# Two-block transformer forward pass in split fp32, one core: the attention bias masked once in its table, and the end of the second block's mixer in another order

## What is computed

```python
for l in range(DEPTH):                                   # first block, DEPTH = 2
    x = x + 0.5 * swiglu(rms_norm(x, ffn1_norm[l]), ffn1_w_in[l], ffn1_w_out[l])
    x = x + mixer(rms_norm(x, mix_norm[l]), ...)         # neighbourhood attention + Fourier mix
    x = x + 0.5 * swiglu(rms_norm(x, ffn2_norm[l]), ffn2_w_in[l], ffn2_w_out[l])

# in the neighbourhood attention: a learned bias per head and offset, and a mask by column
s = einsum(q, k_win) * scale + bias
s = where(col_ok, s, -inf)

for l in range(DEPTH):                                   # second block
    y_a = mla_attention(...)                             # group 0
    y_b = short_gated_conv(...)                          # group 1
    y_c = multiscale_pool(...)                           # group 2
    y_d = swa_sink_attention(...)                        # group 3
    gf = groups * rsqrt(mean(groups * groups) + eps)     # one mean per group of 256 channels
    x = x + (gf * mix_norm) @ w_o[l]
    x = x + (silu(gate) * up) @ w_down[l]
```

## Time and profile before

| | |
|---|---|
| three runs | 1720.05, 1720.64, 1723.21 us, median 1720.64 |
| profiled execution, first to last instruction | 1721.5 us |
| PE busy | 1671.8 us (97%) |
| DVE busy | 943.5 us (55%) |
| ACT busy | 803.8 us (47%) |
| POOL busy | 97.1 us (6%) |
| mean granted TensorE clock | 0.990 |

### The profile page before, as it was taken

How to read it: one execution, slowest core, us unless ns; L and a number is a source line. 1 busy time by engine, 2 the same in 40 slices (tenths; PEclk the granted TensorE clock), 3 DMA queues, 4 the chain that set the end, 5 groups by cost and what they waited for, 6 DMA issues and landing times.

```text
span 1721.5 us, 22066 instructions
## 1 busy us (share of the span) xinstructions
PE 1671.8 (97%) x7760; PEld 1376.7 (80%) x7760; DVE 943.5 (55%) x843; ACT 803.8 (47%) x899; POOL 97.1 (6%) x105
## 2 busy tenths in 40 slices
PE   6999999999999999999999999899999999999998
PEld 5887887888888787888888888787888878788886
DVE  4545545575545645465566545566554556665454
ACT  5443454544434543444455444465444446544443
POOL 2010000010000002000001000021100002110000
PEclk9999999999999999999999999999999999899999
DMA  8875453446565578555345655644456564336552
GB/s 259 295 221 175 172 190 123 139 156 199 176 208 188 175 251 240 174 173 181 111 152 166 203 188 194 240 127 129 141 190 200 179 195 144 125 127 201 189 192 89
DMA packets 209187, 308.96 MB, mean 179 GB/s; under 512 B 10400, under 2 KB 153504, under 8 KB 208480
## 3 DMA queue, kind: packets, MB, share of 16 engines
q1 hardware_dynamic: 208272, 305.18, 54.1%
q0 software_dynamic: 560, 1.84, 0.4%
q10 hardware_dynamic: 288, 1.05, 0.2%
HBM read 306.97 MB, written 2.88 MB: 180 GB/s over the span
## 4 chain that ended last, share of the span: by engine, by line
PE 90%; DVE 3%; ACT 3%; issue 2%; DMA 1%; POOL 1%; DVEq 0%; SPq 0%; ACTq 0%; POOLq 0%
PE pg L1380 19%; PE pg L1381 18%; PE pg L1382 18%; PE acc L1382 9%; PE acc L1380 9%; PE acc L1381 9%; PE pg L1451 2%; DVE wlo L970 2%; ACT whi L671 1%; DMA raw<-in_ffn_w_in 1%; PE pg L1393 1%; PE acc L1530 1%; PE acc L1550 1%; POOL ms L590 0%; PE acc L1538 0%
## 5 line engine op out<-in xcount | busy, mean ns | idle before, releaser
L970 DVE TENSOR_TENSOR wlo<-raw,whi 128x2048 fp32r<-128x2048 f32 x277 | 641.2, 2316 | 513.8 <-ACT whi L671 513.8
L671 ACT ACTIVATE whi<-raw 128x2048 fp32r<-128x2048 f32 x277 | 529.5, 1913 | 338.6 <-PE pg L1382 168.2
L1380 PE MATMUL pg<-whi,xTh 128*128 128x512 f32 (+1 forms) x1456 | 580.3, 399 | 9.9 <-DVE wlo L970 5.7
L1382 PE MATMUL pg<-whi,xTl 128*128 128x512 f32 (+1 forms) x1456 | 570.4, 392 | 0.0
L1381 PE MATMUL pg<-wlo,xTh 128*128 128x512 f32 (+1 forms) x1456 | 570.2, 392 | 0.0
L1380 PEld LDWEIGHTS pg<-whi,xTh 128*128 128x128 f32 x1456 | 276.3, 190 | 73.6 <-DVE wlo L970 9.8
L1382 PEld LDWEIGHTS pg<-whi,xTl 128*128 128x128 f32 x1456 | 276.0, 190 | 57.5
L1381 PEld LDWEIGHTS pg<-wlo,xTh 128*128 128x128 f32 x1456 | 276.5, 190 | 54.3
L1380 PE MATMUL acc<-whi,bTh 128*128 128x512 f32 (+1 forms) x572 | 229.6, 401 | 0.0
L1382 PE MATMUL acc<-whi,bTl 128*128 128x512 f32 (+1 forms) x572 | 224.3, 392 | 0.0
L1381 PE MATMUL acc<-wlo,bTh 128*128 128x512 f32 (+1 forms) x572 | 223.1, 390 | 0.0
(11 more groups left out here) (159 smaller groups left out, 1048.2 us busy)
## 6 DMA issues: line engine op xcount, KB each, us to landing
raw<-in_ffn_w_in SPq DMA_DIRECT2D x176, 512.0 KB, 4.8
raw<-in_ffn_w_out SPq DMA_DIRECT2D x88, 512.0 KB, 4.0
raw<-in_w_gate_up SPq DMA_DIRECT2D x88, 512.0 KB, 4.7
raw<-in_mix_w_in SPq DMA_DIRECT2D x64, 512.0 KB, 4.1
raw<-in_w_down SPq DMA_DIRECT2D x44, 512.0 KB, 4.0
raw<-in_w_in SPq DMA_DIRECT2D x24, 512.0 KB, 4.8
raw<-in_mix_w_o SPq DMA_DIRECT2D x16, 512.0 KB, 4.7
raw<-in_w_o SPq DMA_DIRECT2D x16, 512.0 KB, 4.5
```

The costliest lines, as they stand in the source:

```text
L671: act_e.activation(whi[:, slot, :], raw[:, slot, :], ACT.Copy).then_inc(s.w_hi_ready, 1)
L970: v.tensor_tensor(wlo[:, slot, :], raw[:, slot, :], f32(whi[:, slot, :]), ALU.subtract).then_inc(s.w_lo_ready, 1)
L1380: pe.matmul(dst, xh, wh, start=first and i == 0, stop=False)
L1382: mm = pe.matmul(dst, xl, wh, start=False, stop=last and i == len(pairs) - 1)
```

## The change

The column mask is added to the table `rpb_spread` in memory, once for both layers, by seven more software DMAs that add while they write (`mask_table`). GpSimd issues them after the first norm. SP waits for them before it copies the window, and DVE now waits for the copy itself. GpSimd's addition in SBUF is gone from both layers.

In the second block's mixer the order is changed on all engines. PE attends `sw` unit 2 ahead of `pool_mix`, transposes `pair_T(0, 0)` inside half block 7 and `pair_T(0, 1)` inside `project(0, 0)`, and attends `mla` unit 2 behind `project(0, 0)`. ACT and DVE follow: the refill of unit 12 moves from the front of the `mla` exp to behind `pair_hi(0, 1)`, `scale_pair` is taken tile by tile, and `mla_out(1)` comes behind the refill of unit 12. The transposes of k = 0 use other PSUM banks.

```diff
 def attention_bias():
-    sp.wait_ge(s.rpb_spread, LOADED * NA_DR)
+    sp.wait_ge(s.rpb_masked, LOADED * NA_DR)
...
+def mask_table():
+    mask = bass.AP(tensor=a["consts_a"].tensor, offset=CA_MASK, ap=[[0, DEPTH * NA_H], [CA_COLS, GRID_W], [1, GRID_W]])
+    pool.wait_ge(s.rpb_spread, LOADED * NA_DR)
+    for dr in range(NA_DR):
+        pool.dma_start(spread[:, :, dr * GRID_W:(dr + 1) * GRID_W].rearrange("q h k -> h q k"), mask,
+                       accum_op=ALU.add).then_inc(s.rpb_masked, LOADED)
 spread_table()
+norm(0)
+mask_table()
...
-    pool.wait_ge(s.bias_landed, 64 * l + 64)
-    pool.wait_ge(s.consts_a_landed, 16 * l + 16)
-    pool.tensor_tensor(flat, flat, consts_a[:, CA_MASK:].unsqueeze(1).to_broadcast([P, TT * NA_H, T]),
-                       ALU.add).then_inc(s.bias_masked, 1)
...
 # ACT, end of mixer_b
 group_square(0, 3, 0, s.sw_o_sb, 2 * l + 1)
+group_square(1, 3, 1, s.sw_o_sb, 2 * l + 2)
 refills(11)
-group_square(1, 2, 0, s.pool_sb, l + 1)
-group_square(2, 2, 1, s.pool_sb, l + 1)
+group_square(2, 2, 0, s.pool_sb, l + 1)
+group_square(3, 2, 1, s.pool_sb, l + 1)
 mla_probs_T(1)
-group_square(3, 3, 1, s.sw_o_sb, 2 * l + 2)
-refills(12)
+group_square(4, 0, 0, s.mla_o_sb, 2 * l + 1)
+pair_hi(0, 0)
 mla_exp(2)
 out_gate_copy(1)
 mla_probs_T(2)
-group_square(4, 0, 0, s.mla_o_sb, 2 * l + 1)
-pair_hi(0, 0)
 pair_hi(0, 1)
+refills(12)
+group_square(5, 0, 1, s.mla_o_sb, 2 * l + 2)
 refills(13)
-group_square(5, 0, 1, s.mla_o_sb, 2 * l + 2)
...
 # DVE, end of mixer_b
 mla_out(0)
+sw_out(1)
 (pool scale)
 refills(11)
-sw_out(1)
+scale_pair(0, 0)
 mla_max(2)
+scale_pair(0, 1)
+pair_lo(0, 0)
+conv_in(1)
+pair_lo(0, 1)
 refills(12)
-conv_in(1)
-scale_pair(0)
 mla_out(1)
-pair_lo(0, 0)
-pair_lo(0, 1)
 refills(13)
 (conv gate)
-scale_pair(1)
+scale_pair(1, 0)
+scale_pair(1, 1)
 refills(14)
 pair_lo(1, 0)
```

More of the change, by code:

```diff
@@ L142, in __init__ @@
         self.rpb_spread = sem("rpb_spread")
+        self.rpb_masked = sem("rpb_masked")
         self.bias_landed = sem("bias_landed")
@@ L416, in build, with pair_bank @@
         pairs_b = ((2, 3), (0, 1))
-        def pair_bank(t):
-            return (acc[2], pg[1][0])[t]
+        def pair_bank(k, t):
+            return ((pg[1][0], acc[1]), (acc[2], pg[1][0]))[k][t]
         out_b = ((pg[0][0], acc[3]), (acc[1], acc[0]))
@@ L608, in spread_table @@
                             .then_inc(s.rpb_spread, LOADED)
+            def mask_table():
+                mask = bass.AP(tensor=a["consts_a"].tensor, offset=CA_MASK, ap=[[0, DEPTH * NA_H], [CA_COLS, GRID_W], [1, GRID_W]])
+                pool.wait_ge(s.rpb_spread, LOADED * NA_DR)
+                with nc.allow_non_contiguous_dma(reason="rows of 64 keys"):
+                    for dr in range(NA_DR):
+                        pool.dma_start(spread[:, :, dr * GRID_W:(dr + 1) * GRID_W].rearrange("q h k -> h q k"), mask,
+                                       accum_op=ALU.add).then_inc(s.rpb_masked, LOADED)
             pool.wait_ge(raw_landed[1], 2 * LOADED)
             spread_table()
+            norm(0)
+            mask_table()
             with pool.Fori(0, DEPTH) as l:
-                norm(3 * l)
-                pool.wait_ge(s.bias_landed, 64 * l + 64)
-                pool.wait_ge(s.consts_a_landed, 16 * l + 16)
-                flat = bias.rearrange("p t h k -> p (t h) k")
-                pool.tensor_tensor(flat, flat, consts_a[:, CA_MASK:].unsqueeze(1).to_broadcast([P, TT * NA_H, T]),
-                                   ALU.add).then_inc(s.bias_masked, 1)
                 norm(3 * l + 1)
@@ L625, in _ @@
                 norm(3 * l + 2)
-            norm(6)
+                norm(3 * l + 3)
             with pool.Fori(0, DEPTH) as l:
@@ L899, in pair_hi @@
                     act_e.wait_ge(s.tr_done, 4 * (o + 1) + 2 * k + t + 1)
-                    act_e.activation(xTh[:, 4 * half:4 * half + 4, tok(t)], pair_bank(t)[:, :].rearrange("p (c n) -> p c n", c=4),
+                    act_e.activation(xTh[:, 4 * half:4 * half + 4, tok(t)], pair_bank(k, t)[:, :].rearrange("p (c n) -> p c n", c=4),
                                      ACT.Copy).then_inc(s.xT_hi_ready, 1)
@@ L1081, in mixer_a @@
                 refills(7)
-                v.wait_ge(s.bias_masked, l + 1)
+                v.wait_ge(s.bias_landed, 64 * l + 64)
                 v.wait_ge(s.gate_bias_landed, 32 * l + 32)
@@ L1279, in conv_in, with scale_pair @@
                         .then_inc(s.z_ready, 1)
-                def scale_pair(k):
+                def scale_pair(k, t):
                     v.wait_ge(s.grstd_ready, 2 * l + k + 1)
[L1284 to L1289, removed]
+                    for i, g in enumerate(pairs_b[k]):
+                        c = slice(g * GD, (g + 1) * GD)
+                        last = v.scalar_tensor_tensor(xn[:, t, c], y[:, t, c], g_r[:, k, 2 * t + i:2 * t + i + 1], gain_m[:, c],
+                                                      ALU.mult, ALU.mult)
+                    last.then_inc(xn_ready[t], 1)
                 def pair_lo(k, t):
@@ L1294, in pair_lo @@
                     v.wait_ge(s.xT_hi_ready, 4 * (o + 1) + 2 * k + t + 1)
-                    v.tensor_tensor(xTl[:, part, tok(t)], pair_bank(t)[:, :].rearrange("p (c n) -> p c n", c=4),
+                    v.tensor_tensor(xTl[:, part, tok(t)], pair_bank(k, t)[:, :].rearrange("p (c n) -> p c n", c=4),
                                     f32(xTh[:, part, tok(t)]), ALU.subtract).then_inc(s.xT_lo_ready, 1)
@@ L1321, in mixer_b @@
                 refills(11)
[L1322 removed]
+                v.wait_ge(s.gain_m_landed, 16 * (DEPTH + 1) + 16 * l + 16)
+                scale_pair(0, 0)
                 mla_max(2)
+                scale_pair(0, 1)
+                pair_lo(0, 0)
+                conv_in(1)
+                pair_lo(0, 1)
                 refills(12)
[L1325 to L1327 removed]
                 mla_out(1)
[L1329 to L1330 removed]
                 refills(13)
@@ L1786, in pool_mix, with pair_T @@
                     mm.then_inc(s.unit_done, 1)
+                def pair_T(k, t):
+                    half = 1 - k
+                    if k == 0 and t == 0:
+                        pe.wait_ge(s.z_ready, 2 * l + 1)
+                        pe.wait_ge(s.out_gate_sb, 2 * l + 1)
+                    if k == 0 and t == 1:
+                        pe.wait_ge(s.sw_biased, 3 * l + 3)
+                    pe.wait_ge(xn_ready[t], 2 * (o + 1) + k + 2)
+                    for c in range(4):
+                        at = (4 * half + c) * P
+                        tr = pe.transpose(pair_bank(k, t)[:, c * P:(c + 1) * P], xn[:, t, at:at + P], ident[:, :])
+                    tr.then_inc(s.tr_done, 1)
                 for i in range(8):
@@ L1791, in mixer_b @@
                     u = (6, 9)[b] + half
-                    mm = half_block(t, half, u % SLOTS, rnd + u // SLOTS, BANK, pg[b][t], sw_operands if i == 0 else None)
+                    mm = half_block(t, half, u % SLOTS, rnd + u // SLOTS, BANK, pg[b][t],
+                                    {0: sw_operands, 7: lambda: pair_T(0, 0)}.get(i))
                     if t == 1:
@@ L1817, in mixer_b @@
                         mla_attend(0)
+                        sw_attend(2)
                         pool_mix()
                     if i == 6:
-                        sw_attend(2)
                         mla_probs_T(1)
@@ L1825, in mixer_b @@
                         mla_probs_T(2)
[L1826 to L1838, removed]
                 def project(i, t, amid=None):
@@ L1849, in project @@
                         mm.then_inc(s.mixb_t0_done, 1)
-                pair_T(0, 0)
-                pair_T(0, 1)
-                project(0, 0)
+                project(0, 0, lambda: pair_T(0, 1))
+                mla_attend(2)
                 conv()
```

1 line of the change is left out of this document (removed).

## The result

The changed kernel takes 1724.65 us (median of 20 runs, 1722.06 to 1727.46), the kernel before 1721.76 in the runs beside them (20, 1719.17 to 1724.07). The ratio is 1.0016, 95% interval 1.0009 to 1.0023: 2.8 us slower, where 12.3 us faster was forecast. So the two profiles differ by a gain of 1.3 us where the medians differ by a loss of 2.8.

What follows compares the result with a forecast made beforehand. PE, busy 97% of the span, was taken as the bound. Feed-forward mask 7.0, minus 0.3 for the mask in memory, plus 5.6 at the mixer's end gives 12.3 us: 1720.6 to 1708.3 us, range 1703.5 to 1713.5.

Steps and rivals of the forecast that it cites:

- the mask in memory: Seven adding DMAs near 26 us: 7 to 21 us of all queues, weight loads barely delayed, 0.3 us lost (0 to 2.3).
- sign of being wrong: Prediction wrong if SP stands at the table, an early refill waits long for weights, or PE waits for refill 12 or 13.
- SP's wait: SP first needs the masked table at 104.79 us, 78 us after the adding DMAs start, so its wait costs nothing.
- The rival on the slower side: Adding DMAs hold SP ahead of weight loads; every us past 104.8 starves PE, about 1728 us at 135; chance 0.04.
- The refill: First feed-forward stages: without GpSimd's mask, DVE refills of 6.13 and 5.26 us take 2.29; 7.0 us won.
- slow for another reason: Rival: the feed-forward refills are not slow because of GpSimd, so dropping its mask does nothing; 1715.3 us, chance 0.04.
- The mixer's end: Second block's mixer: new order removes PE's old waits, adds two for pair 1; 2.8 us won per layer, 5.6 together.
- one fall of the clock: Mixer's end: one half-clock stretch expected in one of the two layers, giving 5.6 us; none 7.1, one in both 4.1.
- The rule on small rows: Skill asks 512 B descriptors; mask rows have 256 B. By it the queue takes about twice as long, the sum unchanged.

Runs made afterwards that it cites:

- the packed source: Changed kernel plus one DMA that first copies the mask's block packed into memory, where the seven adding DMAs read it; 1714.26 us, 0.9951 of the kernel before.
- the order alone: Changed kernel with the mask put back on GpSimd in each layer, so only the new order at the mixer's end remains; 1718.82 us, 0.9973 of the kernel before.
- the mask in pieces: New order, no mask in memory, GpSimd's mask instruction cut into 8 of 2 heads each; 1712.46 us, 0.9945 of the kernel before.

## Why the prediction was wrong

- **Where it failed: the mask in memory.** The failing step is the one that takes "0.3 us lost, nearer to nothing, since the queues leave a fifth of the engines unused", with bounds of 0 and 2.3. In its place the runs show 14.5 us (0.9932 to 1.0016); in the profile it is 10.7 us against the kernel before and 11.9 against the one without these DMAs. The source was not looked at: the time was scaled from the spread ("one to three times that, 7 to 21 us"), as if the shape of the target said everything, and 11.2 of the 14.5 us hang on the source. The share of the queue does not show this. Queue 0 rises from 0.4% to 1.7% of the span, some 22 us of all engines and so close to the upper bound of 21, and it shows the same 1.7% with the packed source, where the loss is 3.3 us. But even with this price the step was too sure. By the prediction's own numbers the queues had 67.5% and 14.0% of 50 us; 21 us more is another 42%, together 124%, and the step spoke of a fifth unused. Such a sum is a warning and not a price: packets of two queues can be in flight at once, and the measured shares of the two queues from 10 to 60 us are 99.5% in the changed kernel and 113.9% with the packed source, which loses less. The prediction's sign of being wrong, a refill of the first 60 us that waits long for its weights, is what came: 10.13 us.
- **SP's wait.** Right that the table is no obstacle to SP: the last issue was over near 36 us, and no adding DMA took more than 44.6 us to land, so the table was complete by 81 us, well ahead of SP's copy. The rival on the slower side named the right DMAs and the wrong way. It let them hurt only through this wait, above 115 us, and so gave them 0.04. The loss went through the weights in flight, at once.
- **The refill.** Right, in mechanism and size: 7.0 us forecast, 7.1 measured (0.9973 to 0.9932, some 3 us either way), 7.7 in the lateness above. The rival "slow for another reason" is out. The rule of the Trainium skill ("SBUF — State Buffer", Who interferes with whom) agrees: no refill of the changed kernel is slow beside DMAs (2.31 us at most), and with GpSimd's work in pieces DVE loses 0.2 to 0.4 us.
- **The mixer's end.** Right in its waits: 1.26 us before `pair_T(1, 0)` (1.3 forecast), 1.19 before `project(2, 0)` (1.6 forecast), none before `project(0, 0)`. One more stood close: with the order alone and with the mask in pieces, where the clock stayed full behind `pool_mix` of layer 0, PE waits 0.84 and 0.83 us there before `pair_T(0, 0)`, which was forecast without a wait. The term was 5.6 us for one fall of the clock and 4.1 for one in both layers; both layers had one, and it measured 4.5 in the profile and 4.6 (2.9 to 6.4) in the runs. The refills of 12 and 13 are the late chain, as argued: moving the gate out from behind refill 13 removes the wait.
- **The rule on small rows.** The prediction set the Trainium skill's "DMA: Bandwidth & Descriptors" (Specifications) against the spread and said that by it "the sum would be the same, since nothing waits". The runs show rows of 256 bytes copied at no cost that can be measured (0.9936 against 0.9932), and the same rows at 21 us. So the length of the row is not the cause. Another entry of that page (section Latency and other measured facts) says that a row pitch of a large power of two slows DMA copies from and to memory, with figures for 512 KiB and more, and that padding by 4 KiB restored the rate where 192 bytes did not. Here the pitch is 4 KiB, it takes repeated rows besides, and 256 bytes of padding were enough (0.9936 against 1.0058).
- **What stays open.** What in the memory makes 64 rows at multiples of 4096 bytes slow when seven DMAs read them over and over was not tried further, nor whether 2048 or 8192 do the same, nor whether the number of reads or the number of DMAs decides. That the runs show 14.5 us and the profile 11.9 fits the choice of the execution: it is the fastest of 20 and 2.6 us under its median. Where in the kernel the slower ones lose these 2.6 us was not profiled.

## What to carry to other kernels

Before a DMA is called hidden, add its share, at the upper bound of its price, to the shares of the queues in that stretch. A sum near or over 100% does not say how much is lost (113.9% went with 3.3 us here, 99.5% with 14.5), but it forbids calling the loss nothing while weights are in flight. Look at the source as well as the target: a few rows at multiples of 4096 bytes that several DMAs read again and again (step 0 in the pattern) want to be packed, padded or read once. Where a long GpSimd instruction holds up a two-input one of DVE, first cut it into pieces in its place; here this left PE no wait, like moving the addition away, and cost no transfers.

## What the runs showed of the hardware

- The same seven copies of 1.84 MB cost no time that can be measured with the source's rows 4352 bytes apart, and 21 us with 4096 (landing 4.7 against 18.2 us, all DMAs together 299 against 83 GB/s between 40 and 60 us). Each alone is harmless: rows packed and read 112 times (0.9936), or 7168 different rows 4096 bytes apart (0.9937). Read 16 times by one DMA each they land in 6.7 us.
- An adding DMA of rows of 256 bytes moves one packet for about each row: 7280 packets for seven, against 560 for the plain form. GpSimd needs 9.35 us to issue them where it needs 5.5 for the plain ones. From a packed source they cost 3.3 us here.

```profile
26.91 9.35 POOL L616 DMA_DIRECT2D rpb_spread<-in_consts_a  x7 [1.63 <-DMA rpb_spread<-in_na_rpb]
```

- From the slow source the adding form hurts less than the plain one (1.0016 against 1.0048), though it has 13 times the packets.
- A GpSimd instruction of 9.03 us cut into eight holds DVE up for 0.2 and 0.4 us instead of 3.84, and takes 14.71 us itself.
